# The end of two mixers: turning the first merged columns inside the last merge block, two output tiles ahead of the other turns, and low parts on VectorE only

## The chip, the cores and the metric

One Trainium2 chip, one NeuronCore. The engines are TensorE (matmuls and transposes), VectorE, ScalarE, GpSimd and SyncE, whose queue starts the weight loads. The metric is the time of one launch on the device, in microseconds (us).

## The reference, cut to what matters

The kernel computes ten stages over 256 tokens of width 1024: four gated feed-forward blocks, an attention and a retention layer, and then, twice, a mixer and an MLP. The change lies in the mixers. All matmuls are in float32.

```python
gates = jax.nn.sigmoid((gate_logits + b_gate[l]).reshape(B, S, N_BRANCHES, D))
merged = gates[:, :, 0] * y_diff + gates[:, :, 1] * y_mla + gates[:, :, 2] * y_mem
x = x + merged @ w_out[l]

u = rmsnorm(x, g_mlp[l]) @ w_mlp1[l]
x = x + jnp.square(jax.nn.relu(u)) @ w_mlp2[l]
```

`y_diff`, `y_mla` and `y_mem` are the outputs of three attentions, each multiplied by a matrix of its own (`w_diff_o`, `w_mla_o`, `w_cross_o`).

## The kernel before, in words

**Products in three matmuls.** A float32 product is made of three matmuls in the fast format: high part of x by high part of w, high by low, low by high. The low part is what the high part left out. Each weight tile is 128 by 1024 numbers. SyncE's queue loads it (`w_raw`), ScalarE makes its high part (`w_hi`, L1810), and VectorE (L2090) or GpSimd (L2754) its low part (`w_lo`). There are four buffers of each. ScalarE waits for the matmuls of the tile four places back; the load of a raw buffer waits for the low part of the tile that was in it. With `self.share` at 2 the tiles of even number get their low part on GpSimd, with 0 none does. The mixer sets it to 2 when its attention heads begin, and the next stage sets it back to 0.

**The transposed operand.** The other side of a matmul is a transposed activation. A turn is four transposes of 128 by 128 into one bank of PSUM (L1618), a copy by ScalarE that keeps the high part (`xt_hi`, L1838), and a subtraction by VectorE (`xt_lo`, L2118). The matmuls of a chunk wait for the low part. The tokens are in two halves of 128, so 512 columns take two turns.

**One plan for all engines.** A generator writes one list of steps. Every engine goes through the list in order and issues its part of each step, behind waits on semaphores. What comes first in the plan so comes first in each engine's queue. After the matmuls of tile i (`mm`) the plan has the step that splits tile i+4 (`tile_used`), so ScalarE's and VectorE's queues hold that split at this place. `hold_last` puts off the splits from a stage's last tile on, until the next stage releases them. `second_part` is a pair of a tile count and a function: when that many tiles are planned, the function plans its steps right behind that tile's split.

**The mixer's end.** `merge` runs three times, for `w_diff_o` (8 tiles), `w_cross_o` (4) and `w_mla_o` (4). Each goes over two blocks of 512 columns. After a block VectorE multiplies each half by its gate (L2712, L2718) and from the second merge on adds it to `mx_merged` (L2723). After the third merge the plan before turns the merged columns: first 0 to 511 for both halves, then 512 to 1023, and then come the eight tiles of `w_out`. `last_plain` does these; VectorE adds the result to x (L2195) at the start of the next stage, where `feed` multiplies by a gain (L2098), turns the first 512 columns, runs two tiles, and turns the others.

Of the kernel before, what the change touches and what calls it, by code (L numbers as in the profile page):

```python
# [16 lines left out]
P = 128  # L17
SEQ = 256
HALVES = SEQ // P
# [95 lines left out]
def column_blocks(n, start=0):  # L115
    return [(start + c, min(BLOCK, n - c)) for c in range(0, n, BLOCK)]
# [255 lines left out]
def drive(main, side=None, every=1, finish=True, steps=1):  # L372
    n = 0
    while True:
        try:
            next(main)
        except StopIteration as stop:
            result = stop.value
            break
        n += 1  # L380
        if side is not None and n % every == 0:
            for _ in range(steps):
                next(side, None)
    if side is not None and finish:
        for _ in side:
            pass
    return result


class Kernel:  # L390
# [850 lines left out]
    def mix(self, layer, _):  # L1241
        a, L, small = self.a, f"{layer}", self.small_of
# [39 lines left out]
        def projections():  # L1282
            part = lambda name, dst, after=(): self.project(self.xt, w_in, D, IN_SIZES[name], dst, IN_AT[name], after)
            got["cq"] = yield from part("cq", low[:, :, 0:MLA_QL], self.tok_after[0])
            got["ckv"] = yield from part("ckv", low[:, :, CKV_AT:D], self.tok_after[0])
            got["q"] = yield from part("dq", q)
            for c0, m in column_blocks(D):
                got["k", c0] = yield from self.block(self.xt, w_in, D, IN_AT["dk"] + c0, m)
            got["v"] = yield from part("dv", v)
            yield from need("low_t", "ckt")  # L1290
            got["mq"] = yield from self.project(low_t, a["w_mla_qb_2"][layer], MLA_QL, MLA_H * MLA_QK, mq)
            got["kv"] = yield from self.project(low_t, a["w_mla_kvb_2"][layer], MLA_KVL, MLA_H * PER_KV, kv, first=MLA_QL // P)
            got["low", "over"] = self.last_tile()
            got["xq"] = yield from part("xq", xq, [got["low", "over"]])
            yield from need("qt")
            yield from gate(0)
            yield from need("kt")
            yield from gate(1)
            yield from need("cqt", "mkt")
            yield from gate(2)  # L1300
            self.xt_after = [self.last_tile()]
            yield from merge(0, 0, diff_t, "w_diff_o_2", D, 0)
            yield from merge(1, 2, mc_t, "w_cross_o_2", CROSS_H * CROSS_D, 4)
            yield from merge(2, 1, mc_t, "w_mla_o_2", MLA_H * MLA_V, 0)
# [7 lines left out]
            self.step("next_gain", gi + 2, [("gate_bias", layer, g, HALVES - 1, D - BLOCK)])  # L1312

        merged = self.put("mx_merged" + L, 24, [P, HALVES, D])

        def merge(n, g, xt, name, rows, first):
            while any((int(xt is mc_t), first + i) not in turned_out for i in range(rows // P)):
                yield IDLE
            for half in range(HALVES):
                self.step("sigmoid", layer, g, half, gates[g][:, half, :])  # L1320
            for c, (c0, m) in enumerate(column_blocks(D)):
                b = yield from self.block(xt, a[name][layer], rows, c0, m, first)
                for half in range(HALVES):
                    self.step("merge", layer, n, half, c, b, merged[:, half, c0:c0 + m], gates[g][:, half, c0:c0 + m], g)
# [164 lines left out]
        prepared = together(memory_keys(), diff_keys(), diff_queries(), latent(), latent_keys(), cross_queries(), diff_outputs())  # L1489
        side = self.in_step(prepared, outputs())  # L1490
        drive(projections(), side, finish=False)
        merged_t = Transposed("merged" + L, *self.xt_parts)

        for c in range(2):
            for half in range(HALVES):
                self.turn(lambda h, s: merged[:, h, s * P:(s + 1) * P], merged_t, half, [(4 * c + j, 4 * c + j) for j in range(4)],
                          [("merged", layer, half, c)], self.xt_after)
        self.tok_after = [[("turned", self.uid)]] * HALVES
        drive(self.last_plain(merged_t, a["w_out_2"][layer], D))


# [1408 lines left out]
```

## Time and profile before

| | |
|---|---|
| median of three runs | 2509.88 us (2506.9 to 2510.97) |
| profiled execution, its own time | 2508.46 us |
| its span, first to last instruction | 2507.2 us |
| TensorE, matmuls | 2401.9 us, 96% |
| VectorE | 1483.1 us, 59% |
| ScalarE | 1188.7 us, 47% |
| GpSimd | 285.4 us, 11% |
| low parts on VectorE, on GpSimd | 688, 56 |

The profile is of one execution. The engine names in its rows are PE for TensorE, PEld for its weight loads, DVE for VectorE, ACT for ScalarE, POOL for GpSimd and SP for SyncE. A duration of a matmul is from its start to its modelled end; matmuls overlap, so the pace is read from one start to the next. Times of the trace count from the start of the span. The first mixer ends near 1745 us, the second near 2292.

### The profile page before, as it was taken

The numbers are of one execution on the slowest core, as the hardware profiler recorded it, in microseconds if no ns is written. First come the engines' busy times: TensorE is split into PE (matmuls) and PEld (weight loads), VectorE is DVE, ScalarE is ACT, GpSimd is POOL, SyncE is SP. The second block draws the span as 40 slices with busy tenths as digits, with TensorE's granted clock in tenths as the row PEclk, the third lists the DMA queues.
The fourth block names the chain that finished last, engine by engine and source line by source line (L and its number), as shares of the span: only waits on it lengthen the run. The fifth ranks groups of instructions, "written<-read, shape, count | busy, mean of one in ns | idle before, by whom it ended". The sixth has DMA issues, their size and how long they took to land.

```text
span 2507.2 us, 29698 instructions
## 1 busy us (share of the span) xinstructions
PE 2401.9 (96%) x11806; PEld 1943.9 (78%) x11806; DVE 1483.1 (59%) x2158; ACT 1188.7 (47%) x1754; POOL 285.4 (11%) x248
## 2 busy tenths in 40 slices
PE   6998999989999999999999998999999998999999
PEld 5786777768878877777787786787787876887787
DVE  4545556675555557666555577655665586656653
ACT  4444454344444436444444454554554455554543
POOL 1100010000000000000001121333100122333000
PEclk9999999999999999999999999999999999999999
DMA  6755544446556655544566554435556553445554
GB/s 209 206 178 160 169 127 137 133 150 182 180 168 190 179 184 171 175 141 151 177 181 189 181 171 130 118 125 167 179 177 201 177 165 116 118 143 160 176 176 143
DMA packets 211338, 411.35 MB, mean 164 GB/s; under 512 B 13690, under 2 KB 26890, under 8 KB 211200
## 3 DMA queue, kind: packets, MB, share of 16 engines
q1 hardware_dynamic: 204192, 388.55, 51.0%
q0 software_dynamic: 6576, 19.80, 2.9%
q8 instruction: 93, 1.52, 0.2%
q10 hardware_dynamic: 432, 1.11, 0.1%
q14 instruction: 45, 0.37, 0.0%
HBM read 408.31 MB, written 1.10 MB: 163 GB/s over the span
## 4 chain that ended last, share of the span: by engine, by line
PE 76%; DVE 14%; ACT 6%; issue 2%; DMA 1%; POOL 1%; ACTq 0%; DVEq 0%; POOLq 0%
PE banks L1565 23%; PE banks L1567 22%; PE banks L1566 22%; DVE w_lo L2090 3%; ACT w_hi L1810 3%; PE banks L1618 2%; PE banks L1680 1%; PE banks L1633 1%; ACT probs L1897 1%; DVE mx_merged L2723 1%; DVE probs L2235 1%; PE banks L1665 1%; PE banks L1589 1%; DMA small<-in_diff_lambda 1%; DVE norm_sums L2523 1%
## 5 line engine op out<-in xcount | busy, mean ns | idle before, releaser
L2090 DVE TENSOR_TENSOR w_lo<-w_raw,w_hi 128x1024 fp32r<-128x1024 f32 x688 | 839.2, 1224 | 811.8 <-ACT w_hi L1810 808.1
L1810 ACT ACTIVATE w_hi<-w_raw 128x1024 fp32r<-128x1024 f32 (+2 forms) x744 | 779.5, 1052 | 783.5 <-PE banks L1567 731.2
L1565 PE MATMUL banks<-w_hi,xt_hi 128*128 128x512 f32 (+3 forms) x2112 | 843.7, 399 | 23.7 <-DVE w_lo L2090 9.8
L1566 PE MATMUL banks<-w_lo,xt_hi 128*128 128x512 f32 (+3 forms) x2112 | 819.8, 388 | 0.0
L1567 PE MATMUL banks<-w_hi,xt_lo 128*128 128x512 f32 (+3 forms) x2112 | 819.6, 388 | 0.0
L1565 PEld LDWEIGHTS banks<-w_hi,xt_hi 128*128 128x128 f32 x2112 | 401.1, 190 | 114.4 <-issue 17.2
L1567 PEld LDWEIGHTS banks<-w_hi,xt_lo 128*128 128x128 f32 x2112 | 399.9, 189 | 88.0
L1566 PEld LDWEIGHTS banks<-w_lo,xt_hi 128*128 128x128 f32 x2112 | 401.1, 190 | 82.0 <-issue 3.1
L2735 POOL TENSOR_TENSOR stat<-stat,minus_half 128x1 f32<-128x1 f32 (+2 forms) x60 | 54.5, 914 | 1054.2 <-DVE stat L2177 730.6
L2754 POOL TENSOR_TENSOR w_lo<-w_raw,w_hi 128x1024 fp32r<-128x1024 f32 x56 | 134.0, 2393 | 297.7 <-ACT w_hi L1810 297.6
L1565 PE MATMUL banks<-w_hi,ffn_ht_hi 128*128 128x512 f32 x352 | 141.3, 401 | 3.7 <-DVE w_lo L2090 3.7
L1567 PE MATMUL banks<-w_hi,ffn_ht_lo 128*128 128x512 f32 x352 | 140.1, 398 | 0.0
L1566 PE MATMUL banks<-w_lo,ffn_ht_hi 128*128 128x512 f32 x352 | 140.1, 398 | 0.0
L1565 PE MATMUL banks<-w_hi,mlp_ht_hi 128*128 128x512 f32 x256 | 102.3, 399 | 3.1 <-DVE w_lo L2090 3.1
L1567 PE MATMUL banks<-w_hi,mlp_ht_lo 128*128 128x512 f32 x256 | 101.5, 396 | 0.0
L1566 PE MATMUL banks<-w_lo,mlp_ht_hi 128*128 128x512 f32 x256 | 101.4, 396 | 0.0
L1565 PEld LDWEIGHTS banks<-w_hi,ffn_ht_hi 128*128 128x128 f32 x352 | 66.6, 189 | 19.8 <-DVE w_lo L2090 4.2
L1567 PEld LDWEIGHTS banks<-w_hi,ffn_ht_lo 128*128 128x128 f32 x352 | 66.7, 190 | 16.3
L1566 PEld LDWEIGHTS banks<-w_lo,ffn_ht_hi 128*128 128x128 f32 x352 | 66.8, 190 | 15.7
L1897 ACT ACTIVATE probs<-probs,mx_nmax 128x256 f32<-128x256 f32 x96 | 42.9, 448 | 71.0 <-DVE mx_nmax L2235 70.7
L1838 ACT ACTIVATE xt_hi<-banks 128x512 fp32r<-128x512 f32 x44 | 24.9, 599 | 74.4 <-PE banks L1618 74.4
L1565 PEld LDWEIGHTS banks<-w_hi,mlp_ht_hi 128*128 128x128 f32 x256 | 48.2, 188 | 14.8 <-DVE w_lo L2090 3.5
(384 smaller groups left out, 2530.7 us busy)
## 6 DMA issues: line engine op xcount, KB each, us to landing
w_raw<-in_w_mlp SPq DMA_DIRECT2D x128, 512.0 KB, 3.7
w_raw<-in_w_in SPq DMA_DIRECT2D x104, 512.0 KB, 3.7
w_raw<-in_ffn_w_gate SPq DMA_DIRECT2D x88, 512.0 KB, 3.8
w_raw<-in_ffn_w_up SPq DMA_DIRECT2D x88, 512.0 KB, 3.8
w_raw<-in_ffn_w_down SPq DMA_DIRECT2D x88, 512.0 KB, 3.7
w_raw<-in_attn_w_in SPq DMA_DIRECT2D x72, 512.0 KB, 3.7
w_raw<-in_ret_w_in SPq DMA_DIRECT2D x64, 512.0 KB, 3.8
w_raw<-in_ret_w_out SPq DMA_DIRECT2D x16, 512.0 KB, 4.2
```

The lines of the kernel that those rows point to most:

```text
L1565: pe.matmul(bank, xh, wh, start=(c == 0), stop=False)
L1566: pe.matmul(bank, xh, wl, start=False, stop=False)
L1567: mm = pe.matmul(bank, xl, wh, start=False, stop=(c == b.chunks - 1))
L1589: pe.matmul(bank, xh, hi[:, cols], start=(t.k0 == 0), stop=False)
L1618: mm = pe.transpose(bank[:, j * P:(j + 1) * P], src(t.half, s), order)
L1633: mm = pe.transpose(bank[0:z.shape[-1], at:at + P], z, order)
L1665: mm = pe.transpose(bank[:, (2 * kh + s) * P:(2 * kh + s + 1) * P], p[:, s * SEQ + kh * P:s * SEQ + (kh + 1) * P], k.ident[:, :])
L1810: act.activation(k.w_hi[i % SPLIT][:, 0:m], k.raw[i % RAW][:, 0:m], ACT.Copy).then_inc(*ev.mark(k.w_hi_made, ("w_hi", i)))
L1897: act.activation(row, row, ACT.Exp, bias=h.nmax[:, s:s + 1], scale=-1.0, accum_out=h.den[:, s:s + 1]).then_inc(*done)
L2090: dve.tensor_tensor(lo, raw, hi.bitcast(F32), ALU.subtract).then_inc(*ev.mark(k.w_lo_made, ("w_lo", i)))
L2735: pool.tensor_tensor(out, mean, k.minus_half[:, 0:n], ALU.pow).then_inc(*ev.mark(k.pool_done, name))
L2754: pool.tensor_tensor(lo, raw, hi.bitcast(F32), ALU.subtract).then_inc(*ev.mark(k.w_lo_pool, ("w_lo", i)))
```

## The change

The turns of the merged columns move. Those of columns 0 to 511 are planned behind the first of the two tiles of the last block of the third merge. Those of columns 512 to 1023 are planned behind the second tile of the output projection, which needs only the first four chunks until then. `self.share` is set to 0 in `merge`, so that from the first merge on no low part of the mixer is made on GpSimd.

```diff
         merged = self.put("mx_merged" + L, 24, [P, HALVES, D])
+        merged_t = Transposed("merged" + L, *self.xt_parts)
+
+        def merged_turned(c):
+            for half in range(HALVES):
+                self.turn(lambda h, s: merged[:, h, s * P:(s + 1) * P], merged_t, half, [(4 * c + j, 4 * c + j) for j in range(4)],
+                          [("merged", layer, half, c)], self.xt_after)
+            self.tok_after = [[("turned", self.uid)]] * HALVES

         def merge(n, g, xt, name, rows, first):
             while any((int(xt is mc_t), first + i) not in turned_out for i in range(rows // P)):
                 yield IDLE
             for half in range(HALVES):
                 self.step("sigmoid", layer, g, half, gates[g][:, half, :])
+            self.share = 0
             for c, (c0, m) in enumerate(column_blocks(D)):
+                if n == 2 and c == 1:
+                    self.second_part = len(self.tiles) + 1, lambda: merged_turned(0)
                 b = yield from self.block(xt, a[name][layer], rows, c0, m, first)
...
         drive(projections(), side, finish=False)
-        merged_t = Transposed("merged" + L, *self.xt_parts)
-
-        for c in range(2):
-            for half in range(HALVES):
-                self.turn(lambda h, s: merged[:, h, s * P:(s + 1) * P], merged_t, half, [(4 * c + j, 4 * c + j) for j in range(4)],
-                          [("merged", layer, half, c)], self.xt_after)
-        self.tok_after = [[("turned", self.uid)]] * HALVES
+        self.second_part = len(self.tiles) + 2, lambda: merged_turned(1)
         drive(self.last_plain(merged_t, a["w_out_2"][layer], D))
```

## Rows read from the trace of the kernel before

**Rows 1.** The page, busy time of each engine over the span
```profile
PE 2401.9 (96%) x11806; PEld 1943.9 (78%) x11806; DVE 1483.1 (59%) x2158; ACT 1188.7 (47%) x1754; POOL 285.4 (11%) x248
```

**Rows 2.** Waits of TensorE, whole span: total us, times, longest
```profile
PE banks L1618 <- DVE mx_merged L2723: 6.7, 6, 1.8
```

**Rows 3.** Timeline of TensorE, layer 0: start, duration, form, idle before it
```profile
1733.45 0.39 PE L1565 MATMUL banks<-w_hi,mx_mc_t_hi 128*128 128x512 f32 x1
...
1736.03 0.40 PE L1567 MATMUL banks<-w_hi,mx_mc_t_lo 128*128 128x512 f32 x1
...
1742.40 0.78 PE L1565 MATMUL banks<-w_hi,xt_hi 128*128 128x512 f32 x1
...
1744.95 0.40 PE L1565 MATMUL banks<-w_hi,xt_hi 128*128 128x512 f32 x1
```

**Rows 4.** Table of stretches: length, busy time (count) by engine, granted clock, DMA
```profile
1742.00:1748.00 6.00, 6.00 (x24) 4.88 (x23) 2.06 (x4) 1.66 (x2) 0.25 (x1) 0.77 0.09 32
...
1365.00:1371.00 6.00, 5.87 (x19) 4.65 (x20) 4.98 (x17) 4.05 (x7) 0.56 (x1) 0.72 0.72 229
...
1890.00:1896.00 6.00, 6.00 (x26) 4.86 (x27) 5.88 (x15) 3.88 (x7) 1.14 (x1) 1.00 0.71 236
```

**Rows 5.** Timeline of TensorE, the same place in layer 1
```profile
2282.92 0.40 PE L1567 MATMUL banks<-w_hi,mx_mc_t_lo 128*128 128x512 f32 x1
...
2289.28 0.78 PE L1565 MATMUL banks<-w_hi,xt_hi 128*128 128x512 f32 x1
...
2291.02 0.40 PE L1566 MATMUL banks<-w_lo,xt_hi 128*128 128x512 f32 x1
```

**Rows 6.** Timeline of the other engines, 1730 to 1742
```profile
1730.90 1.06 ACT L1810 ACTIVATE w_hi<-w_raw 128x1024 fp32r<-128x1024 f32 x1 [1.71 <-PE banks L1567]
...
1732.14 1.21 DVE L2090 TENSOR_TENSOR w_lo<-w_raw,w_hi 128x1024 fp32r<-128x1024 f32 x1
...
1733.28 0.68 DVE L2718 TENSOR_TENSOR tmp<-banks,mx_gate 128x512 f32<-128x512 f32 x1
...
1734.85 2.38 POOL L2754 TENSOR_TENSOR w_lo<-w_raw,w_hi 128x1024 fp32r<-128x1024 f32 x1 [3.19 <-ACT w_hi L1810]
...
1735.32 2.47 DVE L2723 TENSOR_TENSOR mx_merged<-mx_merged,tmp 128x512 f32<-128x512 f32 x1
...
1738.85 0.68 DVE L2718 TENSOR_TENSOR tmp<-banks,mx_gate 128x512 f32<-128x512 f32 x1
1739.56 0.69 DVE L2723 TENSOR_TENSOR mx_merged<-mx_merged,tmp 128x512 f32<-128x512 f32 x1
...
1740.88 0.69 DVE L2723 TENSOR_TENSOR mx_merged<-mx_merged,tmp 128x512 f32<-128x512 f32 x1
```

**Rows 7.** GpSimd's low parts, 1690 to 1775: count, ns min/median/max, first and last start
```profile
L2754 POOL TENSOR_TENSOR w_lo<-w_raw,w_hi x12: 2377/2400/2419, 1694.2 to 1764.5; 128x1024 fp32r<-128x1024 f32 x12
```

**Rows 8.** Timeline of TensorE at two pairs of turns, x8
```profile
1698.85 1.03 PE L1618 MATMUL banks<-ident,tok 128*128 128x128 f32 x8
1699.64 0.48 PE L1565 MATMUL banks<-w_hi,mx_diff_t_hi 128*128 128x512 f32 x1
...
1776.01 0.47 PE L1565 MATMUL banks<-w_hi,xt_hi 128*128 128x512 f32 x1 [1.07 <-DVE xt_lo L2118]
```

**Rows 9.** Timeline where the stage behind the first mixer begins
```profile
1763.41 1.06 ACT L1810 ACTIVATE w_hi<-w_raw 128x1024 fp32r<-128x1024 f32 x1 [1.74 <-PE banks L1567]
...
1764.89 2.59 DVE L2098 TENSOR_TENSOR tok<-x,gain 128x512 f32<-128x512 f32 x1
...
1767.54 0.66 PE L1618 MATMUL banks<-ident,tok 128*128 128x128 f32 x4 [0.98 <-DVE tok L2098]
1768.23 0.48 PE L1565 MATMUL banks<-w_hi,xt_hi 128*128 128x512 f32 x1
```

**Rows 10.** Timeline of TensorE, two longer waits elsewhere in the span
```profile
1365.13 0.50 PE L1565 MATMUL banks<-w_hi,ffn_ht_hi 128*128 128x512 f32 x1 [3.72 <-DVE w_lo L2090]
...
1889.95 0.50 PE L1565 MATMUL banks<-w_hi,mlp_ht_hi 128*128 128x512 f32 x1 [3.08 <-DVE w_lo L2090]
```

## The prediction

> **What bounds the kernel now.** I read the page's busy line first, then the list of waits of TensorE, then the table of stretches, and last the timelines of the engines around the two ends of a mixer. In the busy line TensorE stands at 96% of the span [rows 1]: a change in other engines' work counts only where TensorE waits. The list of waits has one entry that this change aims at: 6.7 us, in six waits, for the merged sums ahead of their turns [rows 2]. A second place is touched too, the start of the stage behind the mixer.
>
> The reader should see in the timeline of TensorE [rows 3] how the mixer's end runs. Call the four weight tiles of the last merge M0 to M3, the eight of the output projection O0 to O7, and the next stage's P0, P1 and so on. A tile is 12 matmuls that start 0.234 us apart, 2.81 us. M3 starts at 1733.45 and its last matmul at 1736.03, so it ends at 1736.27. Then come four turns of four transposes, each behind a merged half, and O0 starts only at 1742.40. The clock falls meanwhile: the table of stretches has a granted clock of 0.77, a mean between 2.4 GHz and its lower level of 1.2, for 1742 to 1748 [rows 4]. O0's first six matmuls take 2.55 us (1742.40 to 1744.95) instead of 1.40: 1.15 us for the clock. Layer 1 repeats it: last matmul 2282.92, O0 at 2289.28, fifth matmul of O0 at 2291.02, so 1.74 us for four in place of 0.94, 0.80 for the clock [rows 5].
>
> From the end of M2 to the start of O2 I therefore count, in layer 0, 1744.95 + 18 x 0.234 = 1749.16, less 1733.45: 15.7 us. In layer 1 it is 2291.02 + 20 x 0.234 = 2295.70, less 2280.34 (2282.92 + 0.234 - 2.81): 15.35 us. Three tiles of work are in it, 8.43 us. The rest, 7.3 and 6.9 us, is turns, waits and clock. No change here can bring more than that, about 14 us for both layers.
>
> **What VectorE's queue does.** VectorE takes its work strictly in the order of the plan, and the low part of tile i+4 is planned right after the matmuls of tile i. So before the sums of the first 512 columns stands the low part of O1, which needs ScalarE's high part of O1, which needs M1 to be over; before the sums of the last columns stands the low part of O3, which needs M3. In the rows [rows 6]: ScalarE begins O1's high part at 1730.90, 0.26 us after M1's end (1733.45 - 2.81 = 1730.64), and takes 1.06; VectorE makes O1's low part from 1732.14 and goes on at 1733.28, 1.14 us later; the first products and sums then run until 1737.79. In the last of them the sum took 2.47 us, from 1735.32 to 1737.79, while GpSimd ran a low part from 1734.85 to 1737.23; a sum without GpSimd beside it takes 0.69. So each GpSimd low part holds up a two-input VectorE operation by about 1.8 us. Undisturbed, a pass over two halves is seen at 1738.85 to 1741.57: the first half is over 1.40 us after the start, the second 2.72 us.
>
> **The change, part by part.** (a) *Low parts.* Twelve low parts per layer, from the fifth tile of the first merge to P2 (all with an even number), go from GpSimd to VectorE [rows 7]. Each costs VectorE 1.14 us and takes one hold-up of 1.8 us away where a sum stood beside it. Per two tiles (5.62 us) VectorE now has 2 x 1.14 + 2.72 = 5.0 us. It keeps up, and the matmuls hide it; if a low part came late, TensorE would lose up to its 1.14 us. The loads wait for VectorE in place of GpSimd, 1.2 us less, and were hidden.
>
> (b) *Turns of columns 0 to 511 after M2.* With GpSimd silent, VectorE is free when O1's high part is over at 1731.96, makes the low part and starts the sums at about 1733.13. The halves are over at 1734.53 and 1735.85. M2 ends at 1733.45, so TensorE, which takes the turns ahead of M3, waits 1.1 us, turns for 0.4, waits 0.9 and turns again: a turn of eight costs 0.79 us of TensorE when nothing waits, 1698.85 to 1699.64 [rows 8]. M3 starts at about 1736.30, 2.85 us after M2's end. What was hidden under M3 is now a pause ahead of it.
>
> (c) *Two tiles ahead of the other turns.* M3, O0 and O1 run without a break, 8.43 us, to 1744.75. The high and low copies of the first turns are over at about 1738.3, before O0. The sums of the last columns follow O3's low part: 1739.1 + 0.26 + 1.06 + 1.14 = 1741.6, and end at 1744.3, in time. But O1's use also plans O5's split ahead of the turns. After O1's end ScalarE takes 0.26 + 1.06 us for O5's high part, VectorE 1.14 for its low part, then the low copy of the first turn takes 0.69, and with some 0.15 to the matmul O2 starts 3.3 us after O1's end, at 1748.05. ScalarE's high copies, 0.6 us each behind O5's high part, lie beside VectorE's work.
>
> From M2's end to O2's start that is 2.85 + 8.43 + 3.3 = 14.6 us, for both layers alike: 1.1 us less than now in layer 0 and 0.75 less in layer 1, together **-1.85**. No clock loss is counted: with the work put between, the pauses are 2.85 and 3.3 us in place of one of 6.1.
>
> (d) *The start of the next stage.* Here the low part of P2 moves. ScalarE's high part of P2 is over at 1764.47, and GpSimd makes its low part from 1764.5 on, while VectorE is in the middle of add, gain, add, gain: the projection is added to x and multiplied by the gain, for two halves [rows 7, 9]. On VectorE the low part stands ahead of these adds: it starts at 1764.50, VectorE goes on at 1765.64, and the four operations, of the shapes of the undisturbed pass above, end 2.72 us later, at 1768.36. Now they end at 1767.48, although the last gain takes 2.59 us beside GpSimd and TensorE waits 0.98 for it. Behind them are the low copy of the first turn and P0, which starts at 1768.23 now and about 0.90 later then. Twice that is **+1.8**.
>
> The sum is -1.85 + 1.8 = -0.05, nothing. The profiled execution took 2508.46 us for a span of 2507.2, 1.4 us under the median of 2509.88; I forecast **2509.8 us**. The bounds: the pauses of (b) and (c) can't be under 0.8 us for a turn of eight, and again 0.8 with the 1.07 us that TensorE waits for the low copy where no split is in the way (1776.01, [rows 8]), 2.7 us; above, a clock loss of 0.80 to 1.15 us can come with each of six pauses.
>
> **Does the clock fall in the new pauses?** Rows of this kernel say both. After a wait of 3.72 us the stretch 1365 to 1371 has 0.72; after one of 3.08 us that of 1890 to 1896 has 1.00 [rows 4, 10]. Mine are 2.85, 3.3 and, at the next stage's start, 3.2 us, each with turns inside. I take no loss, nearer to the second. The Trainium skill (TensorE: Matmul & The Clock Gate, Part 1) says that the throttled clock is the default, that activity releases it, and that the monitor runs free of the kernel, so that the point of change varies by run. By that rule one or two of the six pauses could pay in any run, some 1 to 2 us more than my sum; the trace with one fall and one non-fall for similar waits agrees.
>
> **Rivals.**
> *The clock falls.* All six pauses at up to 1.15 us give +6.9 us, 2516.7, slower by 0.27%. It decides the sign from about five falls on. For it: the falls in both layers now. Against: dense tiles of 8.4 us between the pauses, and the 3.08 us wait without a fall. Two falls are the more likely of its outcomes, 2512.
> *The pauses close.* If the sums and turns were ready in time, as the edit's order of matmuls alone would suggest, the pauses would be those 2.7 us per layer instead of 7.3 and 6.9, and the 0.98 us wait for `tok` would go too: 4.6 + 4.2 + 2.0 = 10.8 us, 2499.0. Against it stands the order on VectorE, which the rows show to be strict. It needs sums that don't queue behind O1's and O3's low parts.
> *VectorE becomes the bound.* If a sum takes 2.5 us for another reason than GpSimd, a pair of tiles needs 6.9 us against 5.62, 1.3 more for some four pairs per layer: about +10 us, 2520. Against it: the quick and slow sums differ only in the GpSimd part beside them.
>
> **How the numbers follow.** Forecast 0.62 (2507 to 2512), clock 0.24 (2511 to 2516.7, a sixth of it past the bound), pauses close 0.09, VectorE bound 0.05. What measurement can tell is about 0.2%, 5.0 us. Nearly all of the forecast and five sixths of the clock case lie within it, leaving some 0.09 faster, 0.82 same, 0.09 slower. The range takes in part of the two cases next to it: 2505.0 to 2514.5.
>
> **What would show it.** Right: two pauses of TensorE, near 2.85 us ahead of M3 and 3.3 ahead of O2, no sum over 0.7 us, 24 low parts fewer on GpSimd, P0's first matmul 3.2 us after O7 instead of 2.3, granted clock 1.00 in between. Wrong: turns that don't wait, a clock under 1.00 after a pause, matmuls of the last merge that wait for low parts, or a next stage that starts earlier.

## The result, and the profile after

| | before | the changed kernel |
|---|---|---|
| median of 21 runs each | 2509.43 us (2506.88 to 2510.97) | 2514.22 us (2509.26 to 2517.69, and one run of 2667.51) |
| ratio, 95% interval | | 1.0017, 1.0011 to 1.0023 |

The change makes the kernel slower by 0.17%, 4.3 us. That is just inside what I had called no change (5.0 us), but its interval excludes zero, and the forecast was 2509.8. The profile taken with this result has a granted clock of 0.848 over its whole span and took 2667.51 us, so the rows here are from a later profile of the same kernel (e1_after below: span 2511.2 us, clock 0.993). Lines of kernel.py are shifted by 4 against before, so L1622 is the turn, L2727 the sum, L2094 the low part on VectorE.

The busy line of the page, beside [rows 1]:

```profile
PE 2400.8 (96%) x11806; PEld 1943.4 (77%) x11806; DVE 1498.2 (60%) x2182; ACT 1188.7 (47%) x1754; POOL 226.7 (9%) x224
```

The 24 low parts are on VectorE, which is busy 15 us more. TensorE's busy time is 1.1 us less while the span is 4.0 us longer, so between these two profiles its idle time grew. The clock does not show in this line: over the whole span it is 0.993 after and 0.992 before, with falls at other places in each. Its part is read at the mixers' ends below. The list of waits of TensorE, beside [rows 2]:

```profile
PE banks L1569 <- DVE xt_lo L2122: 14.6, 13, 2.3
...
PE banks L1622 <- DVE mx_merged L2727: 3.4, 4, 1.1
```

The wait for the sums has halved (6.7 to 3.4 us). In its place TensorE waits for low copies, 14.6 us in 13 waits of which the longest is 2.3; before it was 9.6 us in 9, the longest 1.5. The timeline of three engines at the first mixer's end shows both; it answers to [rows 3] and [rows 6]:

```profile
1731.11 1.23 DVE L2094 TENSOR_TENSOR w_lo<-w_raw,w_hi 128x1024 fp32r<-128x1024 f32 x1 [0.60 <-ACT w_hi L1814]
...
1732.25 0.69 DVE L2722 TENSOR_TENSOR tmp<-banks,mx_gate 128x512 f32<-128x512 f32 x1
1732.33 0.39 PE L1571 MATMUL banks<-w_hi,mx_mc_t_lo 128*128 128x512 f32 x1
...
1733.81 0.63 PE L1622 MATMUL banks<-ident,mx_merged 128*128 128x128 f32 x4 [1.08 <-DVE mx_merged L2727]
1734.30 0.69 DVE L2727 TENSOR_TENSOR mx_merged<-mx_merged,tmp 128x512 f32<-128x512 f32 x1
...
1735.04 0.66 PE L1622 MATMUL banks<-ident,mx_merged 128*128 128x128 f32 x4 [0.61 <-DVE mx_merged L2727]
1735.46 0.47 PE L1569 MATMUL banks<-w_hi,mx_mc_t_hi 128*128 128x512 f32 x1
...
1743.71 0.40 PE L1571 MATMUL banks<-w_hi,xt_lo 128*128 128x512 f32 x1
1743.95 1.04 PE L1622 MATMUL banks<-ident,mx_merged 128*128 128x128 f32 x8
1744.21 1.06 ACT L1814 ACTIVATE w_hi<-w_raw 128x1024 fp32r<-128x1024 f32 x1 [1.75 <-PE banks L1571]
...
1745.30 1.23 DVE L2094 TENSOR_TENSOR w_lo<-w_raw,w_hi 128x1024 fp32r<-128x1024 f32 x1 [0.59 <-ACT w_hi L1814]
1746.44 1.28 DVE L2122 TENSOR_TENSOR xt_lo<-banks,xt_hi 128x512 fp32r<-128x512 f32 x2
1747.27 0.63 PE L1569 MATMUL banks<-w_hi,xt_hi 128*128 128x512 f32 x1 [2.29 <-DVE xt_lo L2122]
1747.69 0.63 PE L1570 MATMUL banks<-w_lo,xt_hi 128*128 128x512 f32 x1
...
1750.99 0.39 PE L1569 MATMUL banks<-w_hi,xt_hi 128*128 128x512 f32 x1
```

M2 ends at 1732.33 + 0.234 = 1732.56 and M3 starts at 1735.46: a pause of 2.90 us, forecast 2.85. M3, O0 and O1 run in 8.49 us. At 1743.95 the eight transposes start; then O5's high part on ScalarE, its low part on VectorE (L2094 at 1745.30), and only behind that the low copies (L2122). O2 starts at 1747.27: 3.32 us, forecast 3.3. Then comes what I had left out: the clock falls. From 1747.27 the matmuls start 0.43 us apart and not 0.234, until 1750.7. The table of stretches, columns as in [rows 4], has that fall in both layers; its third row is the next stage's start in layer 0, where the clock stayed up:

```profile
1747.00:1753.00 6.00, 5.73 (x18) 4.62 (x19) 0.72 (x2) 1.05 (x1) 0.00 (x0) 0.72 0.41 126
2297.00:2303.00 6.00, 5.78 (x19) 4.64 (x20) 0.79 (x3) 1.06 (x1) 0.00 (x0) 0.72 0.41 123
...
1769.00:1775.00 6.00, 5.99 (x27) 4.87 (x28) 4.41 (x6) 1.41 (x2) 0.53 (x1) 1.00 0.06 10
```

The next stage's start, beside [rows 9]: P2's low part is the first row, and the adds and gains stand behind it.

```profile
1764.24 1.23 DVE L2094 TENSOR_TENSOR w_lo<-w_raw,w_hi 128x1024 fp32r<-128x1024 f32 x1 [1.57 <-ACT w_hi L1814]
...
1765.38 0.69 DVE L2199 TENSOR_TENSOR x<-banks,x 128x512 f32<-128x512 f32 x1
1765.46 0.40 PE L1571 MATMUL banks<-w_hi,xt_lo 128*128 128x512 f32 x1
...
1766.85 0.66 PE L1622 MATMUL banks<-ident,tok 128*128 128x128 f32 x4 [1.00 <-DVE tok L2102]
...
1768.18 0.66 PE L1622 MATMUL banks<-ident,tok 128*128 128x128 f32 x4 [0.67 <-DVE tok L2102]
1769.01 0.47 PE L1569 MATMUL banks<-w_hi,xt_hi 128*128 128x512 f32 x1 [0.18 <-DVE xt_lo L2122]
```

O7 ends at 1765.70 and P0 starts at 1769.01: 3.31 us, forecast 3.18, before 2.28.

### The profile page after: what moved, and what is told of

The parts are those of the page before. It is cut to its first block, busy times and chain, and to the rows that moved or that the text cites. A ratio compares the mean times of both kernels' runs of the same rounds, so it can differ in the third digit from the quotient of the medians.

```text
span 2666.2 us, 29698 instructions
## 1 busy us (share of the span) xinstructions
PE 2579.8 (97%) x11806; PEld 2003.6 (75%) x11806; DVE 1501.9 (56%) x2182; ACT 1191.0 (45%) x1754; POOL 227.8 (9%) x224
## 4 chain that ended last, share of the span: by engine, by line
PE 87%; DVE 6%; ACT 4%; issue 1%; DMA 1%; POOL 1%; ACTq 0%; DVEq 0%; POOLq 0%
PE banks L1569 25%; PE banks L1571 25%; PE banks L1570 25%; PE banks L1622 3%; PE banks L1684 2%; ACT w_hi L1814 2%; DVE w_lo L2094 1%; PE banks L1637 1%; PE banks L1781 1%; PE banks L1593 1%; PE banks L1594 1%; PE banks L1595 1%; PE banks L1669 1%; PE banks L1658 1%; DMA small<-in_diff_lambda 1%
## 5 line engine op out<-in xcount | busy, mean ns | idle before, releaser
L2094 DVE TENSOR_TENSOR w_lo<-w_raw,w_hi 128x1024 fp32r<-128x1024 f32 (+1 forms) x712 | 868.8, 1224 | 907.9 <-ACT w_hi L1814 906.3
L1569 PE MATMUL banks<-w_hi,xt_hi 128*128 128x512 f32 (+3 forms) x2112 | 886.4, 420 | 23.2 <-DVE xt_lo L2122 13.3
L1571 PE MATMUL banks<-w_hi,xt_lo 128*128 128x512 f32 (+3 forms) x2112 | 862.3, 408 | 0.0
L1570 PE MATMUL banks<-w_lo,xt_hi 128*128 128x512 f32 (+3 forms) x2112 | 861.9, 408 | 0.0
L1569 PEld LDWEIGHTS banks<-w_hi,xt_hi 128*128 128x128 f32 x2112 | 410.3, 194 | 137.8 <-issue 18.8
L1571 PEld LDWEIGHTS banks<-w_hi,xt_lo 128*128 128x128 f32 x2112 | 408.2, 193 | 112.2
L1570 PEld LDWEIGHTS banks<-w_lo,xt_hi 128*128 128x128 f32 x2112 | 410.3, 194 | 106.6 <-issue 3.9
L1571 PE MATMUL banks<-w_hi,ffn_ht_lo 128*128 128x512 f32 x352 | 147.4, 419 | 0.0
L2758 POOL TENSOR_TENSOR w_lo<-w_raw,w_hi 128x1024 fp32r<-128x1024 f32 x32 | 76.3, 2385 | 218.8 <-ACT w_hi L1814 218.7
L1571 PEld LDWEIGHTS banks<-w_hi,mlp_ht_lo 128*128 128x128 f32 x256 | 49.1, 192 | 15.2
```

The costliest lines, as they stand in the source:

```text
L1569: pe.matmul(bank, xh, wh, start=(c == 0), stop=False)
L1570: pe.matmul(bank, xh, wl, start=False, stop=False)
L1571: mm = pe.matmul(bank, xl, wh, start=False, stop=(c == b.chunks - 1))
L2094: dve.tensor_tensor(lo, raw, hi.bitcast(F32), ALU.subtract).then_inc(*ev.mark(k.w_lo_made, ("w_lo", i)))
L2758: pool.tensor_tensor(lo, raw, hi.bitcast(F32), ALU.subtract).then_inc(*ev.mark(k.w_lo_pool, ("w_lo", i)))
```

## The experiments

Twelve kernels ran. Three of them are earlier ones again, for a second profile. A fall of the clock is a stretch in which TensorE is granted the lower level. In this table "length" is the time from M2's end to P2's first matmul, both layers added, from each kernel's profile; it holds both merged ends and both starts of the next stage. Before it is 84.8 and 85.2 us in two profiles. The pauses are those ahead of M3, ahead of O2 and ahead of P0, in layer 0, turns included; where the turns stand ahead of O0, the pause there is given. "Falls" counts those of the clock in this length, out of both layers.

| kernel | ratio to before, interval | median, us | M3 | O2 | P0 | falls | length, us |
|---|---|---|---|---|---|---|---|
| before, two profiles | 1 | 2509.5 | | 6.1 (O0) | 2.28 | 2, 2 | 84.8, 85.2 |
| e1, e10: the change | 1.0019, 1.0010 to 1.0028 | 2514.33 | 2.90 | 3.32 | 3.3 | 2, 3 | 88.3, 89.5 |
| e2: share alone | 1.0020, 1.0011 to 1.0029 | 2516.02 | | 6.1 (O0) | 3.33 | 4 | 90.2 |
| e3: turns alone | 1.0040, 1.0027 to 1.0052 | 2520.28 | 5.0 | 3.4 | 2.28 | 4 | 93.3 |
| e4: P2 on GpSimd | 1.0011, 1.0002 to 1.0019 | 2512.96 | 2.88 | 3.33 | 2.28 | 2 | 86.4 |
| e5: turns ahead of O5 | 0.9999, 0.9991 to 1.0008 | 2509.29 | 2.89 | 2.11 | 3.33 | 0 | 82.9 |
| e6, e11: sums ahead of O1 | 1.0000, 0.9991 to 1.0009 | 2509.22 | 1.06 | 3.32 | 3.33 | 0, 2 | 81.7, 84.7 |
| e7: P2 behind the turns | 1.0001, 0.9992 to 1.0010 | 2510.56 | 2.88 | 3.33 | 2.10 | 2 | 86.0 |
| e8: everything | 0.9962, 0.9950 to 0.9975 | 2500.09 | 1.06 | 0.79 | 2.11 | 0 | 74.2 |
| e9: e8 with GpSimd | 0.9971, 0.9959 to 0.9982 | 2501.92 | 1.89 | 0.80 | 2.10 | 0 | 75.8 |

**e1_after**, the changed kernel unedited.

> The changed kernel again, for a profile in which TensorE's clock is granted in full outside short falls. Theory A (queue order and clock): the pauses are as forecast, 2.85 us ahead of M3, 3.3 ahead of O2, 3.2 at the next stage's start, and the 4.3 us that the change costs come from falls of the clock behind the second and perhaps the third pause, 0.8 to 1.3 us each, two to four of them. Theory B (longer waits): a pause is longer than forecast, or matmuls of the merges wait for low parts on VectorE, and the granted clock around the mixers' ends is no lower than before. Theory C: the ends of the mixers are no longer than before (15.7 and 15.35 us from M2's end to O2's start, 2.3 at the next stage), and the time is lost elsewhere in the span.

The pauses are there to within 0.15 us, and the clock falls behind the second in both layers. Of the 4 us that the span grew from 2507.2 to 2511.2, 3.6 lie between M2 and P2 (88.32 against 84.75). Theory A holds. B falls, since the pauses are those of the forecast and no matmul of the merges waited for a low part; C falls, since the added time lies at the mixers' ends.

**e2_share_only**, the kernel before with one line:

```diff
             for half in range(HALVES):
                 self.step("sigmoid", layer, g, half, gates[g][:, half, :])
+            self.share = 0
```

> Only the low parts leave GpSimd, the turns stay where they were. Theory A: the long pause between M3 and O0 stays at 6.1 us with its fall of clock, since O3's low part stands ahead of the last sums as before; the start of the next stage comes 0.9 us later in each layer, so +1.8 us, 0 to +2 more if the clock falls there: ratio 1.0007 to 1.0015. Theory B: merges wait for low parts, more than +4 us.

A miss in size: 1.0020, where 1.0007 to 1.0015 was expected. The pause ahead of P0 grew by 1.05 us as the mechanism says, and the one between M3 and O0 stayed near 6.0 (6.06 and 5.98, before 6.13). But the clock fell four times: between M3 and O0 as before, and also behind the longer pause at the next stage, in both layers. The table of stretches:

```profile
1769.00:1775.00 6.00, 6.00 (x22) 4.74 (x22) 4.41 (x6) 1.23 (x2) 0.53 (x1) 0.80 0.08 20
...
2321.00:2327.00 6.00, 5.95 (x19) 4.82 (x20) 4.41 (x6) 1.45 (x2) 0.00 (x0) 0.72 0.00 0
```

So taking the low parts off GpSimd is by itself a loss here. Of the 5.2 us by which its length exceeds the mean of the two profiles before, 4.9 lie at P0: 2.1 us of pause and 2.8 us of clock.

**e3_turns_only**, the change without `self.share = 0`.

> Only the turns move, every second low part stays on GpSimd. Theory A: the second sum of columns 0 to 511 is held up by GpSimd's low part to about 4.4 us after M2's end, so M3 starts 4.8 us after M2 instead of 2.85; the next stage starts 2.3 us after O7 as before. Against the change as a whole: +2.0 -0.9 us per layer, +2.2 in all, ratio to before about 1.0025. Theory B: the moved low parts are what costs, so this is no slower than before, 1.000.

The pause ahead of M3 is 5.0 us, expected 4.8, and is made by one held-up sum. The timeline has GpSimd's low part, the sum beside it, and the turn that waits:

```profile
1734.44 2.35 POOL L2757 TENSOR_TENSOR w_lo<-w_raw,w_hi 128x1024 fp32r<-128x1024 f32 x1 [3.17 <-ACT w_hi L1813]
1734.91 2.42 DVE L2726 TENSOR_TENSOR mx_merged<-mx_merged,tmp 128x512 f32<-128x512 f32 x1
...
1737.39 1.02 PE L1621 MATMUL banks<-ident,mx_merged 128*128 128x128 f32 x4 [2.34 <-DVE mx_merged L2726]
```

The turn at 1737.39 took 1.02 us, not 0.66: behind so long a pause the clock was already down, and it fell again at O2's start, in both layers alike. The four falls cost 5.9 us, against 3.0 and 4.3 in the two profiles of the change. The 2.3 us more than their mean are over half of the way from the expected 1.0025 to 1.0040 (3.8 us). Turning early without `self.share = 0` is worse than the whole change: every run of e3 is above every run of e1. Whether e2 is worse than the change can't be told, as the intervals are nearly the same.

**e4_p2_pool**, the change with one low part back on GpSimd:

```diff
-        self.step("split", i, "pool" if self.share and i % self.share == 0 else "dve")
+        self.step("split", i, "pool" if i == self.pool_at or self.share and i % self.share == 0 else "dve")
...
+        self.pool_at = len(self.tiles) + 10
         drive(self.last_plain(merged_t, a["w_out_2"][layer], D))
```

> The change, but the low part of P2 alone goes back to GpSimd. Theory A: the next stage starts 2.3 us after O7 as before instead of 3.2, -1.8 us against the change, and one clock fall per layer less if there was one there (-1 to -2 more): ratio to before 1.0002 to 1.0010. The two pauses at the merged end stay at 2.85 and 3.3 us. Theory B: less than 1 us against the change.

The pause ahead of P0 is 2.28 us as before, and the median 1.4 us under the change's. The ratio of 1.0011 is just above the 1.0010 that was expected at most, and the intervals of e4 and e1 overlap; the length (86.4 against 88.3 and 89.5) shows the gain more clearly.

**e5_turns_before_o5.** In `block`, for the turns of the last columns only:

```diff
             if self.second_part and len(self.tiles) == self.second_part[0]:
-                self.tile_used(used)
-                self.second_part[1]()
+                if self.turns_first:
+                    self.second_part[1]()
+                    self.tile_used(used)
+                else:
+                    self.tile_used(used)
+                    self.second_part[1]()
```

> The change, with the turns of the last columns planned ahead of O5's split instead of behind it. Queue and clock: the pause ahead of O2 falls from 3.3 to 2.1 us in both layers, and the falls of the clock behind it (1.5 and 1.2 us) go away: -2.4 us for the pause and -2.7 for the clock against the change, a ratio to before of 0.9995 to 1.0005. If the falls had another cause than this pause (the pause ahead of M3, or chance), only the 2.4 us go: ratio 1.0005 to 1.0012, slow matmuls still seen after O2's start. If O5's split does not set the pause, nothing changes.

As expected, 0.9999. The pause is 2.11 us, 1744.71 to 1746.82 in the timeline, and no slow matmul stands behind it:

```profile
1744.71 1.04 PE L1628 MATMUL banks<-ident,mx_merged 128*128 128x128 f32 x8
1746.82 0.47 PE L1575 MATMUL banks<-w_hi,xt_hi 128*128 128x512 f32 x1 [1.07 <-DVE xt_lo L2128]
```

Against the change's median that is 5.0 us less: 2.4 for the pauses, and the rest is put down to the clock, whose falls cost 3.0 and 4.3 us in the change's profiles. That none came behind the pauses of 3.32 us ahead of P0 may be chance, as the repeats below show.

**e6_sums_before_o1.** The last tile of the third merge's first block keeps back its `tile_used` until the sums are planned:

```diff
                 for half in range(HALVES):
                     self.step("merge", layer, n, half, c, b, merged[:, half, c0:c0 + m], gates[g][:, half, c0:c0 + m], g)
+                if n == 2 and c == 0:
+                    self.tile_used(self.after_sums)
```

> The change, with the sums of columns 0 to 511 planned ahead of O1's split. Queue and clock: the sums start about 0.4 us after M1's end instead of 2.5, the pause ahead of M3 falls from 2.85 us to about 1.0 in both layers, -3.7 us; the pause of 3.3 us ahead of O2 and the fall of the clock behind it stay: ratio to before 1.0000 to 1.0008. If the pause ahead of M3 shares in bringing the clock down, the slow matmuls behind O2's start go too, -2.7 us more: 0.9990 to 0.9998.

The pause ahead of M3 is 1.06 us, and the ratio 1.0000. Surprising was that no slow matmuls stood behind the pause ahead of O2, though it was 3.32 us as in the change. By this one profile the shorter pause ahead of M3 could be what keeps the clock up; e11 below puts that to the test.

**e7_p2_behind.** `last_plain` holds the splits one tile earlier, and `feed` releases P2's behind its first turns:

```diff
             first()
+            if len(self.held) > 1:
+                self.release(1)
             self.second_part = len(self.tiles) + 2, second
```

> The change, with P2's split planned behind the next stage's first adds and turns, still on VectorE. Queue and clock: P0 starts about 2.1 us after O7's end instead of 3.3, -2.4 us against the change; the falls behind O2's start stay: ratio to before 1.0006 to 1.0012. If the low part in itself were the cost and not its place, nothing changes, 1.0017.

The pause ahead of P0 is 2.10 us. The median lies 3.8 us under the change's, where the pauses give 2.4; the ratio of 1.0001 is under the 1.0006 that was expected at least, though the interval reaches there. Pauses of 2.1 us had no fall in any profile, those of 3.3 us at this place had one in five of twelve, so part of the difference is the clock's.

**e8_all.** e5, e6 and e7 together, the sums ahead of O3's split too, and the turns of the last columns behind O0 instead of O1:

```diff
+        self.second_part = len(self.tiles) + 1, lambda: merged_turned(1)
+        self.turns_first = True
+        drive(self.last_plain(merged_t, a["w_out_2"][layer], D, 1))
```

> All of it: sums ahead of the splits of O1 and O3, the turns of the last columns right behind O0 and ahead of its split, P2's split behind the next stage's first turns, no low parts on GpSimd. Queue and clock: the two pauses at the merged end are about 1.0 us each, of which 0.8 is turns, no fall of the clock there; the next stage starts 2.1 us after O7. Against before -5.3 and -4.9 us at the two merged ends and -0.4 at the next stages: -10 us, ratio 0.9955 to 0.9965. If VectorE runs late with the low parts behind the sums, TensorE waits for w_lo at O1 or O3 and the gain is under 5 us.

2500.09 us, 0.9962: the version that beats both kernels. Both turns cost TensorE hardly more than the transposes (pauses of 1.06 and 0.80 us, of which a turn of eight takes 0.79), since the sums are ready in time and a tile runs between each turn and the first matmul that needs it. From the timeline of TensorE:

```profile
1731.77 1.31 PE L1635 MATMUL banks<-ident,mx_merged 128*128 128x128 f32 x8
1732.83 0.48 PE L1582 MATMUL banks<-w_hi,mx_mc_t_hi 128*128 128x512 f32 x1
...
1738.51 1.04 PE L1635 MATMUL banks<-ident,mx_merged 128*128 128x128 f32 x8
1739.30 0.48 PE L1582 MATMUL banks<-w_hi,xt_hi 128*128 128x512 f32 x1
```

**e9_all_gpsimd**, the same without `self.share = 0`.

> The version with everything, but with every second low part left on GpSimd as in the kernel before. If GpSimd's low parts hold up VectorE's two-input operations for up to 1.8 us each where sums are due, the pauses at the merged end grow by 0.5 to 2 us per layer: ratio to before 0.9965 to 0.9978 against 0.9962. If the order of the queue is all that mattered, no change against the version with everything, 0.9962, to within 0.0004.

The pause ahead of M3 is 0.83 us longer. GpSimd's low part holds up a sum of the second merge, and everything behind it on VectorE is late:

```profile
1729.35 0.68 DVE L2734 TENSOR_TENSOR tmp<-banks,mx_gate 128x512 f32<-128x512 f32 x1
1729.68 2.40 POOL L2770 TENSOR_TENSOR w_lo<-w_raw,w_hi 128x1024 fp32r<-128x1024 f32 x1 [3.26 <-ACT w_hi L1826]
1730.07 2.56 DVE L2739 TENSOR_TENSOR mx_merged<-mx_merged,tmp 128x512 f32<-128x512 f32 x1
...
1735.21 1.22 DVE L2106 TENSOR_TENSOR w_lo<-w_raw,w_hi 128x1024 fp32r<-128x1024 f32 x1
1735.26 3.43 POOL L2770 TENSOR_TENSOR w_lo<-w_raw,w_hi 128x1024 fp32r<-128x1024 f32 x1 [3.18 <-ACT w_hi L1826]
```

0.9971 against 0.9962; the intervals overlap, the profiles differ by 1.6 us in length, all of it in this pause. By the profiles, low parts on VectorE pay once nothing urgent stands behind them; the times alone don't show it.

**e10_after_again, e11_sums_again, e12_before_again**, second profiles of the change, of e6 and of the kernel before.

> The changed kernel a second time, for its profile alone: does the clock fall again behind O2's start in both layers? Queue and clock says yes: 6 to 8 slow matmuls behind a pause of 2.9 us, 8.5 us of matmuls and a pause of 3.3 us. If the falls were chance, one or both are missing.

> The version with the sums ahead of O1's split a second time, for its profile alone: pauses of 1.06 and 3.32 us. If the shorter first pause is what keeps the clock up, again no slow matmuls behind O2's start in either layer; if that was chance, slow ones are seen in one or both.

> The kernel before a second time, for its profile alone. The fall of the clock between M3 and O0 should come in both layers again (0.8 to 1.2 us of slow matmuls each), since the pause of 6.1 us is the same. Behind the wait of 3.1 us near 1890 us the first profile had no fall and the changed kernel's had one of 1.5 us: if that is chance, this profile may have it.

In the change (e10) the clock did not fall behind the pause of layer 0, but did in layer 1, and behind both pauses ahead of P0. The stretches are, in this order, behind the pause ahead of O2 in layer 0, behind the one ahead of P0 in layer 0, and behind the one ahead of O2 in layer 1:

```profile
1744.00:1750.00 6.00, 5.68 (x25) 4.62 (x25) 1.99 (x3) 1.06 (x1) 0.00 (x0) 1.00 0.41 125
1764.00:1770.00 6.00, 5.88 (x22) 4.54 (x20) 4.78 (x7) 1.54 (x2) 0.53 (x1) 0.72 0.01 4
2296.00:2302.00 6.00, 6.00 (x19) 4.78 (x20) 0.69 (x2) 1.06 (x1) 0.00 (x0) 0.72 0.35 102
```

In e11 the pauses equal e6's, and this time layer 1 has a fall behind the pause ahead of O2, at 0.72, and another one ahead of P0; layer 0 has none. The stretches behind the pause ahead of O2:

```profile
1747.00:1753.00 6.00, 5.89 (x25) 4.81 (x26) 1.78 (x2) 1.06 (x1) 0.00 (x0) 1.00 0.37 115
...
2294.00:2300.00 6.00, 6.00 (x20) 4.74 (x21) 1.00 (x2) 1.06 (x1) 0.00 (x0) 0.72 0.38 107
```

In the kernel before (e12) both falls at the mixers' ends came again, and the wait near 1890 us, which had none in [rows 4], had one:

```profile
1743.00:1749.00 6.00, 5.79 (x21) 4.83 (x22) 2.65 (x5) 1.67 (x3) 0.00 (x0) 0.74 0.17 62
...
1892.00:1898.00 6.00, 6.00 (x21) 4.75 (x20) 5.26 (x14) 3.44 (x7) 0.56 (x1) 0.72 0.80 247
```

The first profile was the exception: around 1890 us the granted clock is under 1.00 in 11 of the 13 profiles of all these kernels (not in the first of before and not in e7), and around 1365 us in 12 of 13 (not in e10).

So a pause of about 3.3 us brings the clock down in some executions and not in others; that e6's first profile had no fall does not make its shorter pause a cure.

## Why the prediction was wrong

*What bounds, and the order on VectorE*: right. Each pause stands where it was put, made by the instruction named: O1's low part, O5's split, P2's low part. e5, e6, e7 and e4 moved one each, and the pause followed to within 0.2 us of what its place in the queue gives.

*Part (a), low parts*: right. VectorE kept up, and the sums took 0.69 us. The rival in which VectorE becomes the bound is out.

*Part (b), ahead of M3*: 2.90 us, forecast 2.85. *Part (c), ahead of O2*: 3.32, forecast 3.3. *Part (d), ahead of P0*: 3.31, forecast 3.18, since TensorE waited 0.18 us for the low copy behind the turn.

*The clock*: this is the step that failed, "No clock loss is counted". By pauses alone the merged ends had nothing to gain: 2.85 + 3.3 = 6.15 us against one of 6.13. The whole -1.85 was the clock loss of 1.15 and 0.80 us that I took to be gone. It was not: the falls between M2 and P2 cost 3.0 and 4.3 us in the two profiles of the change, and 1.8 and 2.3 in the two of before, so some 1.6 us more in the mean. The pauses, turns included, are 9.5 us a layer against 8.4, 2.3 us more for both, which is the later P0 for the most part. Together that is 3.9 us of the 4.3 measured.

The same against the sum of the prediction. The change's sizes without it were near: pauses of 2.90, 8.49 for the three tiles, 3.32 and 3.31 us against 2.85, 8.43, 3.3 and 3.18, some 0.3 us a layer. In e5, which has no fall, the length is 41.45 us a layer; with the 1.2 us of pause that it lacks against the change, that is 42.65 us. My sum gives 42.35 for the change (84.76, the two layers before, less 0.05, halved). The change itself has 44.22 and 44.10 in e1, with falls of 1.55 and 1.45 us. So 0.6 us a run come from sizes, and the falls, two and three in the two profiles, give 3.6 in the mean. Together 4.2 us above a forecast of no change; 4.3 were measured. That it comes so near is partly luck, since two profiles are few for an event that comes and goes.

The rival "the clock falls", to which I gave 0.24, is what happened, with two to three falls where I had priced two at 2512. I had let it decide the sign only from about five falls on, since I took 5 us for the least that can be told from no change. Over 21 runs each, 4.3 us was enough to tell.

I had weighed a wait of 3.72 us with a fall against one of 3.08 without, and had gone by the nearer. The second was one draw, and a rare one: 11 of 13 profiles have a fall at this place. Nor are my six pauses alike. Those of 2.9 us ahead of M3 had no fall behind them in any of ten cases (e1, e4, e5, e7, e10), so for these two "no loss" was right. For the four of 3.3 us the runs give 13 falls in 24 cases at 1.3 to 1.6 us each, where I had taken 1.15 for the most; that is about 3.2 us for the four. The sentence from the Trainium skill (TensorE: Matmul & The Clock Gate, Part 1), that the monitor runs free of the kernel so that the point of change varies by run, pointed there, and the traces agree: equal pauses, other falls (13 of 24). I had named "1 to 2 us more" by it and then left it out of the sum.

*The pauses close*: it didn't happen in the change, but e8 shows the condition that I had named for it, sums that don't queue behind O1's and O3's low parts, and it moves the splits behind the second turns and P2's too. It gave 9.4 us where the rival had 10.8. The terms differ: the two pauses at the merged end are 1.9 us a layer where the rival left 2.7, and the pause ahead of P0 got 0.2 us shorter and not 1.0.

What stays open: the medians of the slower versions lie 1 to 2 us above what their length explains (e3: 8.4 us by length, 10.6 measured; e4: 1.4 and 3.3), and e8's gain of 10.8 by length is 9.4 measured. Falls elsewhere in the span come at other places in each profile, so one profile can't settle that. Whether a shorter pause ahead of M3 makes the fall behind the next one rarer is open too: one of four in e6 and e11, seven of eight in e1, e4, e7 and e10. So is why the pauses of 2.9 us had none.

## What to carry to other kernels

Moving a step forward in a common plan moves it on one engine only; on the others it stands behind whatever the plan has ahead of it, here a weight split whose matmuls start 11 us later or more. Ask for each moved step which queue it waits in, and move the non-urgent work behind it as well: the edit gained nothing until that was done, and 0.38% then. The copies behind a turn are hidden only if a tile of matmuls runs between it and its first reader. And for a pause of 3.3 us count half a fall of the clock in a kernel like this one, whatever the one profile at hand shows; at 2.9 us with turns inside none was seen.

## What the runs showed of the hardware

Equal pauses of 3.3 us, turns inside, had a fall to the lower level in 13 of 24 cases over eight profiles (8 of 12 ahead of O2, 5 of 12 ahead of P0), each costing 1.3 to 1.6 us. Pauses of 2.9 us ahead of M3 had none in ten cases, and pauses of 2.1 us at O2 or P0 none in eight. Which of the pauses of 3.3 us have one changes between executions of the same kernel.

GpSimd and VectorE hold each other up in both directions. GpSimd's low part takes 2.40 us and stretched a sum of 0.69 us to 2.42, 2.47 or 2.56 us: each time it ended 0.54 to 0.56 us after GpSimd's own operation. Beside VectorE's low part, which had begun 0.05 us earlier, GpSimd's took 3.43 us itself (e9, the last two rows). A product on VectorE that reads one of its inputs from PSUM was not stretched: the first row of that fence ran 0.35 us of its 0.68 beside GpSimd's low part.
